# Splitting a stream of expert weight loads between two issuing engines: odd units from ScalarE, even units from SyncE

## The chip, the cores and the metric

The kernel runs on one core of one Trainium2 chip. The metric is the device time of one execution in microseconds (us), lower is better. The profiled execution is a separate one, recorded by the hardware profiler; its trace holds every instruction of the five engines and every packet that the core's 16 DMA engines moved.

## What is computed

One encoder layer over 528 tokens (16 meta tokens and 512 of the input) of width 1024: a retention branch and a long-convolution branch are mixed and added to the tokens, and then a mixture of 16 experts with expert choice follows. Each expert takes the 66 tokens for which its router weight is highest. The part that matters here is the experts:

```
xe  = xn[idx]                                        # 16 experts x 66 tokens x 1024
hid = silu(xe @ w_gate[e]) * (xe @ w_up[e])           # 66 x 2048
ye  = (hid @ w_down[e]) * gate[e]                     # 66 x 1024
out = out.at[idx].add(ye)
```

Everything is float32. The three weight matrices of an expert have 2M elements each, so 24 MiB per expert and 384 MiB in all have to come from HBM, once.

## The kernel before

The first half of the kernel (to about 950 us of the profiled execution) is the two branches and the router. The second half is the experts, and the change is there alone.

**Units.** The weights of the experts are cut into units of 2 MiB. An expert has four units of gate weights, four of up weights and four of down weights. A gate or up unit gives each of the 128 partitions two neighbouring rows of 2048 floats, which lie together in HBM (16 KB); a down unit gives each partition four rows of 1024 floats that lie apart (4 KB each). Unit and expert are named (e, c) in the code, with `MOE_CH` = 12 units to a pass: c = 0 to 3 are the gate units of expert e, c = 4 to 7 its up units, and c = 8 to 11 the down units of expert e - 1, since the down product of an expert runs one pass late. The eight gate and up units of expert 0 come before pass 1 (`high_first`, `low_first`), and the four down units of expert 15 behind pass 15, as (E, 0) to (E, 3) with E = 16.

**Slots and casts.** Units land in a ring of `SLOTS` = 6 float32 buffers `slot`, unit (e, c) in slot (c + 2) % 6. Each unit is then split into two float16 parts: ScalarE (ACT) casts it to the high part `wh` (`high`, L640 to L644), VectorE (DVE) forms the low part `wl` from the float32 unit and `wh` (`low`, L982 to L986), and TensorE (PE) multiplies with both. `wh` and `wl` have `RING` = 4 buffers each. The cast of a unit waits for its landing and for PE to be done with the unit four before it. A slot is free when `low` has been through it, which the semaphore `w_lo` counts.

**Who issues the loads.** All unit loads are issued by SyncE (SP) on its hardware DMA queue (q1 in the profile), in the order of the units:

```
def load(e, c, src, rows):
    sp.wait_ge(S["w_lo"], e * MOE_CH + c - SLOTS - 3)
    sp.dma_start(slot_dst(c + 2, rows), src).then_inc(slot_in[(c + 2) % SLOTS], 16)
```

The wait says that `low` has finished the unit six before this one, whose slot the load overwrites. SP does nothing else in this stage.

**What else is in a pass of ACT and DVE.** ACT's program is in order: twelve casts, and between them `silu` (three activations on PSUM, ahead of the cast of c = 7), `ye_out` and `hidt_high` (behind the cast of c = 3), and `evac_x` (behind the cast of c = 11). DVE runs twelve `low`, with `hidt_low` behind c = 3, and `gated` and `split_x` behind c = 11. GpSimd (POOL) issues one gather (`xg`) and one scatter with accumulation (`h_rows`) for each expert on a queue of its own (q0). ACT's own hardware DMA queue (q10) carries five small loads at the start of the kernel and nothing later.

Of the kernel before, what the change touches and what calls it, by code (L numbers as in the profile page):

```python
# [15 lines left out]
E, FF = 16, 2048  # L16
# [54 lines left out]
MOE_CH = 12  # L71
RING = 4
SLOTS = 6
# [106 lines left out]
def build(nc, A, out, xn2_rows, h_rows):  # L180
    ctx = ExitStack()
    with ctx:
# [12 lines left out]
        S = {n: ctx.enter_context(nc.semaphore("s_" + n)) for n in SEMS}  # L195
        raw_in = [ctx.enter_context(nc.semaphore(f"s_raw_in{i}")) for i in range(3)]
        slot_in = [ctx.enter_context(nc.semaphore(f"s_slot_in{i}")) for i in range(SLOTS)]
# [100 lines left out]
        def gate_src(e, q):  # L298
            return w_gate[e].rearrange("(p k) n -> p k n", k=KD)[:, 2 * q:2 * q + 2, :]

        def up_src(e, q):
            return w_up[e].rearrange("(p k) n -> p k n", k=KD)[:, 2 * q:2 * q + 2, :]

        def down_src(e, q):
            return w_down[e].rearrange("(t p) n -> p t n", p=128)[:, 4 * q:4 * q + 4, :]

        def slot_dst(n, rows):
            return slot[n % SLOTS][:, :].rearrange("p (k n) -> p k n", k=rows)
# [4 lines left out]
        def bank_of(b, base=0):  # L313
            return ps_all[:, base + 512 * b:base + 512 * b + TIL * CAP] if b < 2 else ps_all[:, base + 1024:base + 1024 + 4 * CAP]

        def span_of(t, b):
            return t[:, TIL * CAP * b:min(TIL * CAP * (b + 1), 16 * CAP)]
# [3 lines left out]
        @block.sync  # L321
        def _(sp):

            sp.dma_start(htok[0:NMETA, 0, :], A["meta_tokens"]).then_inc(S["h_tok"], 16)
            sp.dma_start(htok[:, 1:NT, :], A["x"][0].rearrange("(k p) d -> p k d", p=128)).then_inc(S["h_tok"], 16)

            def load_chunk(n):
                if n >= 3:
                    sp.wait_ge(S["raw_lo"], n - 2)
                name, c0 = CHUNKS[n]  # L330
                sp.dma_start(raw[n % 3][:, :, :], w[name][:, :, c0:c0 + CW]).then_inc(raw_in[n % 3], 16)

            def load_first(c):
                src = gate_src(0, c) if c < 4 else up_src(0, c - 4)
                sp.dma_start(slot_dst(c, 2), src).then_inc(slot_in[c % SLOTS], 16)

            for n in range(NCH):
                load_chunk(n)
                if n == 1:
                    sp.dma_start(w4[:, :], A["hy_filt_w4"][0]).then_inc(S["filt_params"], 16)  # L340
                    sp.dma_start(win[:, :, :], A["c_win"][:, :, 0, :]).then_inc(S["win"], 16)
                    sp.dma_start(dft_f[:, :, :, :], A["c_dft_f"]).then_inc(S["dft_fwd"], 16)
                    sp.dma_start(dft_i[:, :, :, :], A["c_dft_i"]).then_inc(S["dft_inv"], 16)
                if n == 7:
                    sp.wait_ge(S["tile_done"], AT[("Y", 0, 3)] + 1)
                    sp.dma_start(win[:, :, :], A["c_win"][:, :, 1, :]).then_inc(S["win"], 16)
                if n == 12:
                    sp.wait_ge(S["tile_done"], AT[("Z", 1, NT - 1)] + 1)
                    sp.dma_start(cosT[:, :], A["c_cos"]).then_inc(S["tables"], 16)
                    sp.dma_start(sinT[:, :], A["c_sin"]).then_inc(S["tables"], 16)  # L350
                    sp.dma_start(utab[:, :], A["c_u"]).then_inc(S["tables"], 16)
                if n >= C_A + 1 and n < C_A + 5:
                    if n == C_A + 1:
                        sp.wait_ge(S["yain_split"], KD)
                    load_first(n - C_A - 1)
                if n == C_B + 2:
                    sp.wait_ge(S["tile_done"], AT[("YA", KD - 1)] + 1)
                    sp.dma_start(h[0:NMETA, 0, :], A["meta_tokens"]).then_inc(S["h_again"], 16)
                    sp.dma_start(h[:, 1:NT, :], A["x"][0].rearrange("(k p) d -> p k d", p=128)).then_inc(S["h_again"], 16)
            sp.wait_ge(S["tile_done"], AT[("YB", KD - 1)] + 1)  # L360
            sp.dma_start(g2b[:, :], A["norm2_g"][0].partition_broadcast(128)).then_inc(S["g2_row"], 16)
            sp.wait_ge(S["tile_done"], AT[("WO", 3, NT - 1)] + 1)
            load_first(4)
            load_first(5)
            for c in (6, 7):
                sp.wait_ge(S["w_lo"], c - SLOTS + 1)
                load_first(c)
            sp.wait_ge(S["rows_landed"], 32)
            sp.dma_start(gfb[:, :], A["final_norm_g"].partition_broadcast(128)).then_inc(S["gf_row"], 16)

            def load(e, c, src, rows):
                sp.wait_ge(S["w_lo"], e * MOE_CH + c - SLOTS - 3)
                sp.dma_start(slot_dst(c + 2, rows), src).then_inc(slot_in[(c + 2) % SLOTS], 16)

            with sp.Fori(1, E) as e:
                for q in range(4):
                    load(e, q, gate_src(e, q), 2)
                for q in range(4):
                    load(e, 4 + q, up_src(e, q), 2)
                for q in range(4):  # L380
                    load(e, 8 + q, down_src(e - 1, q), 4)
            for q in range(4):
                load(E, q, down_src(E - 1, q), 4)
            sp.wait_ge(S["rows_landed"], 32 + 16 * E)
            for k in range(1, NT):
                sp.dma_start(hfin[:, k - 1, :], h_rows[TS[k][0]:TS[k][0] + 128, :]).then_inc(h_back[k - 1], 16)
            for k in range(1, NT):
                sp.wait_ge(S["fin_ready"], k)
                sp.dma_start(out[0, 128 * (k - 1):128 * k, :], hfin[:, k - 1, :]).then_inc(S["out_stored"], 16)
            sp.wait_ge(S["out_stored"], 16 * (NT - 1))  # L390
# [72 lines left out]
        def _(act):  # L463
# [162 lines left out]
            def evac_x(e):  # L626

                act.wait_ge(S["xe_done"], e + 1)
                for b in range(2):
                    src = ps_all[:, 1536 + 512 * b:1536 + 512 * b + 4 * CAP].rearrange("p (k c) -> p k c", k=4)  # L630
                    nc.scalar.activation(xcur[:, 4 * b:4 * b + 4, 0, :], src, ACT.Copy).then_inc(S["xcur_hi"], 1)

            def high_first(c):

                act.wait_ge(slot_in[c % SLOTS], 16 * (c // SLOTS + 1))
                if c >= RING:
                    act.wait_ge(S["chunk_used"], c - RING + 1)
                nc.scalar.activation(wh[c % RING][:, :], slot[c % SLOTS][:, :], ACT.Copy, scale=W_S).then_inc(S["w_hi"], 1)  # L638

            def high(e, c):  # L640

                act.wait_ge(slot_in[(c + 2) % SLOTS], e * 32 + 16 * ((c + 2) // SLOTS))
                act.wait_ge(S["chunk_used"], e * MOE_CH + c - RING - 3)
                nc.scalar.activation(wh[c % RING][:, :], slot[(c + 2) % SLOTS][:, :], ACT.Copy, scale=W_S).then_inc(S["w_hi"], 1)  # L644

            def silu(done):

                act.wait_ge(S["chunk_used"], done)
                for b in range(BANKS):
                    nc.scalar.activation(span_of(sg, b), bank_of(b), ACT.Silu, scale=1.0 / W_S).then_inc(S["psum_free"], 1)  # L650
# [5 lines left out]
            def ye_out(e, done, at):  # L656
                act.wait_ge(S["chunk_used"], done)
                act.wait_ge(S["rows_landed"], e * 16 + 32)
                nc.scalar.activation(ye[:, :], ps_all[0:CAP, at:at + 1024], ACT.Copy, scale=gate[:, bass.ds(e, 1)]).then_inc(S["ye_ready"], 1)  # L659
# [6 lines left out]
            for c in range(2, 8):  # L666
                if c == 7:
                    silu(4)
                high_first(c)
            evac_x(1)  # L670

            def moe(e, second, last):

                for c in range(MOE_CH):
                    if c == 7:
                        silu(e * MOE_CH)
                    high(e, c)
                    if c == 3:
                        if not second:
                            ye_out(e - 2, e * MOE_CH - 4, 3072)  # L680
                        hidt_high(e - 1, hidt)
                if not last:
                    evac_x(e + 1)
# [4 lines left out]
            moe(E - 1, False, True)  # L688
            hidt_high(E - 1, hidt_end)
            for c in range(4):  # L690
                high(E, c)
                if c == 3:
                    ye_out(E - 2, E * MOE_CH - 4, 3072)
# [721 lines left out]
```

## Time and profile before

| | before |
|---|---|
| median of 3 runs | 1984.39 us (1984.2 to 1988.61) |
| profiled execution, its own time | 1983.55 us |
| span of the profiled execution | 1981.7 us |
| mean granted TensorE clock | 0.924 of full speed |
| busy share of the span: PE, DVE, ACT, POOL | 82%, 63%, 50%, 13% |
| queue q1 (SP), all loads of the kernel | 467.94 MB |
| expert stage, in the span | about 953 to 1960 us |

Busy shares are averages over both halves. In the expert stage alone DVE and ACT are much busier than the table says, and so are the DMA engines. The span runs from the first instruction to the last one; the profiled execution's own time is 1.85 us more than its span. "DMA share" of a stretch is the mean busy share of the 16 DMA engines, and it can read a little over 1 since packets overlap at their ends.

### The profile page before, as it was taken

The page shows a single profiled execution, that of the slowest core. Times are in us where ns is not written, and L with a number is a line of the kernel's source. Part 1 is how long each engine was busy: PE and PEld are TensorE (multiplying, and loading weights), DVE is VectorE, ACT ScalarE, POOL GpSimd, SP SyncE. Part 2 cuts the span into 40 slices and gives each one's busy share as a digit, 9 for nine tenths or more (in the row PEclk, how much of TensorE's full clock was granted, in tenths as well). Part 3 has the DMA queues.
Part 4 walks back from the last instruction along what each step waited for, and adds up shares of the span by engine and source line. Part 5 has one row for each costly group of instructions (what it writes and reads, how often), then busy time and mean ns, then how long its engine had stood idle before and what let it go on. Part 6 is the DMA issues. An engine that isn't in the chain of part 4 may idle for free.

```text
span 1981.7 us, 43798 instructions
## 1 busy us (share of the span) xinstructions
PE 1625.5 (82%) x19979; PEld 1225.1 (62%) x19979; DVE 1255.5 (63%) x733; ACT 1000.6 (50%) x622; POOL 263.9 (13%) x137
## 2 busy tenths in 40 slices
PE   4898999898999999984568787778876787777974
PEld 3553773487868888873566565655565565654652
DVE  4423343247235233334699888989889988899884
ACT  4231133132213222222487777777677777777763
POOL 0405041403000000000007301101011000101000
PEclk9799999899999999995789899989899999899987
DMA  9000210112200725122799999999999999999993
GB/s 324 22 22 0 77 58 0 64 44 85 86 0 22 291 94 170 54 79 94 311 361 408 402 410 406 408 412 412 402 403 415 409 409 404 404 416 408 422 406 122
DMA packets 107994, 482.43 MB, mean 243 GB/s; under 512 B 5867, under 2 KB 51243, under 8 KB 91212
## 3 DMA queue, kind: packets, MB, share of 16 engines
q1 hardware_dynamic: 102656, 467.94, 60.0%
q0 software_dynamic: 4704, 12.98, 2.4%
q8 instruction: 66, 1.08, 0.2%
q10 hardware_dynamic: 556, 0.32, 0.1%
q14 instruction: 12, 0.10, 0.0%
HBM read 470.48 MB, written 10.75 MB: 243 GB/s over the span
## 4 chain that ended last, share of the span: by engine, by line
PE 37%; DMA 32%; DVE 14%; ACT 9%; issue 6%; POOL 2%; SPq 0%; ACTq 0%; DVEq 0%; POOLq 0%
PE ps_all L1047 23%; DMA slot<-in_w_exp_gate 15%; DMA slot<-in_w_exp_down 15%; DVE wl L985 8%; ACT wh L644 6%; PE ps_all L1070 5%; PE ps_all L1128 4%; DVE tmp L826 1%; PE ps_all L1114 1%; POOL qk L427 1%; PE ps_all L1232 1%; ACT wh L638 1%; POOL tmp L419 1%; POOL psp L424 1%; DMA xg<-xn_rows,tok 1%
## 5 line engine op out<-in xcount | busy, mean ns | idle before, releaser
L985 DVE SCALAR_TENSOR_TENSOR wl<-slot,wh 128x4096 f16<-128x4096 f32 x184 | 809.2, 4422 | 98.9 <-ACT wh L644 98.6
L644 ACT ACTIVATE wh<-slot 128x4096 f16<-128x4096 f32 x184 | 664.3, 3616 | 223.4 <-DMA slot<-in_w_exp_down 104.1
L1269 PE MATMUL ps_all<-xcur,wl 128*128 128x66 f16 x4096 | 421.7, 198 | 183.7 <-ACT sg L650 103.5
L1269 PEld LDWEIGHTS ps_all<-xcur,wl 128*128 128x128 f16 x4096 | 397.5, 102 | 200.1 <-ACT sg L650 105.1
L1270 PE MATMUL ps_all<-xcur,wh 128*128 128x66 f16 x4096 | 421.4, 199 | 6.5 <-issue 6.5
L1271 PE MATMUL ps_all<-xcur,wh 128*128 128x66 f16 x4096 | 420.7, 200 | 6.5 <-issue 6.5
L1270 PEld LDWEIGHTS ps_all<-xcur,wh 128*128 128x128 f16 x4096 | 397.5, 100 | 6.8 <-issue 6.5
L1271 PEld LDWEIGHTS ps_all<-xcur,wh 128*128 128x128 f16 x4096 | 397.6, 101 | 3.1 <-issue 3.1
L1047 PE MATMUL ps_all<-xnt,wsp 128*128 128x272 f16 (+1 forms) x2688 | 309.8, 278 | 7.0 <-DVE rot L860 5.2
L1047 PEld LDWEIGHTS ps_all<-xnt,wsp 128*128 128x128 f16 x2688 | 264.9, 99 | 52.4 <-issue 8.4
L1283 PE MATMUL ps_all<-wh,hidt 128*66 128x512 f16 x480 | 182.6, 380 | 23.7 <-DVE wl L985 23.4
L719 DVE SCALAR_TENSOR_TENSOR wsp<-raw,wsp 128x2048 f16<-128x2048 f32 x44 | 100.8, 2291 | 136.7 <-ACT wsp L477 136.5
L1285 PE MATMUL ps_all<-wh,hidt 128*66 128x512 f16 x480 | 182.6, 380 | 0.0
L1284 PE MATMUL ps_all<-wl,hidt 128*66 128x512 f16 x480 | 182.4, 380 | 0.0
L447 POOL DMA_INDIRECT h_rows<-ye,tok x16 | 97.9, 6117 | 527.4 <-ACT ye L659 527.4
L477 ACT ACTIVATE wsp<-raw 128x2048 f16<-128x2048 f32 x44 | 83.5, 1901 | 78.7 <-PE ps_all L1047 38.0
L1283 PEld LDWEIGHTS ps_all<-wh,hidt 128*66 128x66 f16 x480 | 53.2, 111 | 80.6 <-issue 35.6
L440 POOL DMA_INDIRECT xg<-xn_rows,tok x16 | 36.7, 2296 | 410.7 <-PE ps_all L1252 360.5
L1285 PEld LDWEIGHTS ps_all<-wh,hidt 128*66 128x66 f16 x480 | 53.4, 111 | 50.8 <-issue 0.7
L1284 PEld LDWEIGHTS ps_all<-wl,hidt 128*66 128x66 f16 x480 | 53.4, 111 | 45.9 <-issue 0.7
L1047 PE MATMUL ps_all<-dft_i,psp 128*128 128x272 f16 (+1 forms) x480 | 65.8, 303 | 11.4 <-POOL psp L424 11.4
L1128 PE MATMUL ps_all<-zt_t,dft_f 128*128 128x512 f16 (+3 forms) x300 | 70.6, 386 | 3.5 <-DVE zt_t L815 3.5
(189 smaller groups left out, 1603.3 us busy)
## 6 DMA issues: line engine op xcount, KB each, us to landing
slot<-in_w_exp_gate SPq DMA_DIRECT2D x64, 2048.0 KB, 23.7
slot<-in_w_exp_up SPq DMA_DIRECT2D x64, 2048.0 KB, 21.4
slot<-in_w_exp_down SPq DMA_DIRECT2D x64, 2048.0 KB, 22.6
raw<-in_w_in SPq DMA_DIRECT2D x32, 1024.0 KB, 5.9
raw<-in_w_ret_out SPq DMA_DIRECT2D x4, 1024.0 KB, 13.1
raw<-in_w_hy_out SPq DMA_DIRECT2D x4, 1024.0 KB, 7.7
raw<-in_w_o SPq DMA_DIRECT2D x4, 1024.0 KB, 5.3
dft_f<-in_c_dft_f SPq DMA_DIRECT2D x1, 2640.0 KB, 18.3
```

The lines of the kernel that those rows point to most:

```text
L644: nc.scalar.activation(wh[c % RING][:, :], slot[(c + 2) % SLOTS][:, :], ACT.Copy, scale=W_S).then_inc(S["w_hi"], 1)
L719: nc.vector.scalar_tensor_tensor(wsp[n % 3][:, 1, :, :], raw[n % 3][:, :, :], W_S, wsp[n % 3][:, 0, :, :], ALU.mult, ALU.subtract).then_in ...
L985: nc.vector.scalar_tensor_tensor(wl[c % RING][:, :], slot[(c + 2) % SLOTS][:, :], W_S, wh[c % RING][:, :], ALU.mult, ALU.subtract).then_in ...
L1047: last = nc.tensor.matmul(pair(n, c, c + b - a, p), l, r[:, a:b], start=i == 0, stop=i == len(terms) - 1)
L1070: last = nc.tensor.matmul(pair(n, 0, CW, p), l, r, start=i == 0, stop=i == 3 * KD - 1)
L1128: last = nc.tensor.matmul(pair(n, 512 * a, 512 * a + 512, fp), l, r, start=i == 0, stop=i == 3 * NT - 1)
L1269: nc.tensor.matmul(dst, lo, xcur[:, k, 0, :], start=k == 0 and t % TIL == 0, stop=False, skip_group_check=True)
L1270: nc.tensor.matmul(dst, hi, xcur[:, k, 0, :], start=False, stop=False, skip_group_check=True)
L1271: last = nc.tensor.matmul(dst, hi, xcur[:, k, 1, :], start=False, stop=k == KD - 1, skip_group_check=True)
L1283: nc.tensor.matmul(dst, l[0], wh[i][:, f:f + 512], start=t == 0, stop=False)
L1284: nc.tensor.matmul(dst, l[0], wl[i][:, f:f + 512], start=False, stop=False)
L1285: last = nc.tensor.matmul(dst, l[1], wh[i][:, f:f + 512], start=False, stop=t == 15)
```

## The change

SP issues the loads of even c only. The loads of odd c are issued by ACT, on ACT's own hardware queue, from the middle of its program: ahead of the cast of an odd unit c it issues the load of unit c + 2; ahead of the cast of c = 11 it issues (e + 1, 1), or (E, 1) in the last pass. (1, 1) is issued ahead of the last cast of expert 0's units, behind a `silu`, and (E, 3) ahead of the cast of (E, 1). The slots, the semaphores, the counts waited for, the sources and the sizes are the same as before. DVE's, PE's and POOL's programs are the same.

```diff
             with sp.Fori(1, E) as e:
-                for q in range(4):
+                for q in (0, 2):
                     load(e, q, gate_src(e, q), 2)
-                for q in range(4):
+                for q in (0, 2):
                     load(e, 4 + q, up_src(e, q), 2)
-                for q in range(4):
+                for q in (0, 2):
                     load(e, 8 + q, down_src(e - 1, q), 4)
-            for q in range(4):
+            for q in (0, 2):
                 load(E, q, down_src(E - 1, q), 4)
...
+            def load_odd(e, c):
+                act.wait_ge(S["w_lo"], e * MOE_CH + c - SLOTS - 3)
+                if c < 4:
+                    src, rows = gate_src(e, c), 2
+                elif c < 8:
+                    src, rows = up_src(e, c - 4), 2
+                else:
+                    src, rows = down_src(e - 1, c - 8), 4
+                act.dma_start(slot_dst(c + 2, rows), src).then_inc(slot_in[(c + 2) % SLOTS], 16)
+
+            def load_end(q):
+                act.wait_ge(S["w_lo"], E * MOE_CH + q - SLOTS - 3)
+                act.dma_start(slot_dst(q + 2, 4), down_src(E - 1, q)).then_inc(slot_in[(q + 2) % SLOTS], 16)
...
             for c in range(2, 8):
                 if c == 7:
                     silu(4)
+                    load_odd(1, 1)
                 high_first(c)
...
                 for c in range(MOE_CH):
                     if c == 7:
                         silu(e * MOE_CH)
+                    if c % 2 and c < MOE_CH - 2:
+                        load_odd(e, c + 2)
+                    elif c % 2 and not last:
+                        load_odd(e + 1, 1)
+                    elif c % 2:
+                        load_end(1)
                     high(e, c)
...
             for c in range(4):
+                if c == 1:
+                    load_end(3)
                 high(E, c)
```

## Rows read from the trace of the kernel before

**Rows 1.** Busy time by stretch: us, then each engine's, granted clock, DMA share, GB/s.

```profile
995.00:1004.00 9.00, 2.06 (x38) 2.07 (x39) 6.73 (x2) 9.00 (x3) 0.00 (x0) 0.57 0.47 154
1004.00:1075.00 71.00, 60.97 (x1218) 50.02 (x1216) 71.00 (x23) 60.02 (x25) 25.15 (x2) 0.93 1.00 407
1075.00:1930.00 855.00, 663.52 (x11822) 508.69 (x11819) 759.34 (x246) 633.89 (x258) 99.14 (x26) 0.93 1.01 409
```

**Rows 2.** The chain that ended last, 1075 to 1930 us, by line.

```profile
by line: DMA slot<-in_w_exp_gate 35.8%; DMA slot<-in_w_exp_down 34.6%; DVE wl L985 15.9%; ACT wh L644 11.4%; issue 2.2%; SPq L373 0.2%; DVE hid L993 0.2%; DVE hidt L997 0.1%; ACTq L643 0.1%; ACT hidt_end L654 0.0%
```

**Rows 3.** Costliest groups: busy us, mean ns | idle before, releaser; the cast.

```profile
L644 ACT ACTIVATE wh<-slot 128x4096 f16<-128x4096 f32 x184 | 664.3, 3616 | 223.4 <-DMA slot<-in_w_exp_down 104.1
```

**Rows 4.** ACT in order of time, part of one pass: start, us, instruction, idle before.

```profile
1405.07 3.62 ACT L644 ACTIVATE wh<-slot 128x4096 f16<-128x4096 f32 x1 [1.50 <-DMA slot<-in_w_exp_down]
1410.18 3.62 ACT L644 ACTIVATE wh<-slot 128x4096 f16<-128x4096 f32 x1 [1.49 <-DMA slot<-in_w_exp_down]
1417.76 3.62 ACT L644 ACTIVATE wh<-slot 128x4096 f16<-128x4096 f32 x1 [3.96 <-DMA slot<-in_w_exp_down]
1421.29 0.66 ACT L631 ACTIVATE xcur<-ps_all 128x264 f16<-128x264 f32 x2
1422.82 3.62 ACT L644 ACTIVATE wh<-slot 128x4096 f16<-128x4096 f32 x1 [0.88 <-DMA slot<-in_w_exp_gate]
1427.72 3.62 ACT L644 ACTIVATE wh<-slot 128x4096 f16<-128x4096 f32 x1 [1.28 <-DMA slot<-in_w_exp_gate]
...
1455.71 1.15 ACT L650 ACTIVATE sg<-ps_all 128x396 f32<-128x396 f32 x3
```

**Rows 5.** DVE in order of time: four `low` in a row, and what follows c = 11.

```profile
1015.79 17.43 DVE L985 SCALAR_TENSOR_TENSOR wl<-slot,wh 128x4096 f16<-128x4096 f32 x4
...
1425.75 1.38 DVE L993 SCALAR_TENSOR_TENSOR hid<-ps_all,sg 128x396 f32<-128x396 f32 x3
1427.05 0.76 DVE L974 TENSOR_TENSOR xcur<-ps_all,xcur 128x264 f16<-128x264 f32 x2
```

**Rows 6.** All instructions on `slot`: one load issue (ns), and issue to landing.

```profile
L373 SPq DMA_DIRECT2D slot<-in_w_exp_gate x60: 332/340/4277, 963.3 to 1854.6; - x60
...
DMA to landing us min/median/max: 7.3/22.6/25.6
```

**Rows 7.** DMA packets in 1424 to 1427 us (gate, up), and 1395 to 1400 us (down).

```profile
DMA packets 91, 1.31 MB, mean 437 GB/s; under 512 B 11, under 2 KB 11, under 8 KB 11
...
DMA packets 522, 2.07 MB, mean 415 GB/s; under 512 B 16, under 2 KB 16, under 8 KB 522
```

**Rows 8.** DMA queues in 6.0 to 6.5 us: packets, MB, share of 16 engines.

```profile
q1 hardware_dynamic: 42, 0.17, 88.0%
q10 hardware_dynamic: 36, 0.02, 12.2%
```

**Rows 9.** DMA queues in 1387 to 1390 us.

```profile
DMA packets 130, 1.16 MB, mean 386 GB/s; under 512 B 30, under 2 KB 30, under 8 KB 69
...
q1 hardware_dynamic: 64, 1.00, 78.9%
q0 software_dynamic: 66, 0.16, 27.1%
```

**Rows 10.** ACT in order of time, start of the expert stage.

```profile
973.82 3.63 ACT L638 ACTIVATE wh<-slot 128x4096 f16<-128x4096 f32 x1
...
993.62 14.13 ACT L644 ACTIVATE wh<-slot 128x4096 f16<-128x4096 f32 x4
...
1027.63 14.14 ACT L644 ACTIVATE wh<-slot 128x4096 f16<-128x4096 f32 x4 [0.60 <-PE ps_all L1271]
```

**Rows 11.** ACT, casts of c = 11 in the last two passes.

```profile
1856.57 3.62 ACT L644 ACTIVATE wh<-slot 128x4096 f16<-128x4096 f32 x1 [1.49 <-DMA slot<-in_w_exp_down]
...
1917.35 3.62 ACT L644 ACTIVATE wh<-slot 128x4096 f16<-128x4096 f32 x1 [1.47 <-DMA slot<-in_w_exp_down]
```

## The prediction

> **What bounds the kernel now.** I read the busy time by stretch first. From 1075 to 1930 us the 16 DMA engines are full (share 1.01, 409 GB/s), while the busiest compute engine, DVE, works 759 of 855 us [rows 1]. The chain that ended last agrees: 70% of that stretch is landing of weights, and 27% the low and high split in between [rows 2]. The groups show the cast waiting 223 us, most of it for landings [rows 3]. ACT in order of time shows how tight it is: down units are cast 5.11 us apart, gate units 4.90 us apart, each cast 3.6 us, and the wait of 1.3 to 1.5 us before each is for the landing [rows 4]. So in this stage time is packets divided by what the DMA engines carry, and a change of issuers can do two things: change that rate, or leave the engines without work. Before 1075 us the engines have one gap, 995 to 1004 us (share 0.47) [rows 1], and casts wait for PE.
>
> **What is removed.** SP loses half its issues, 0.34 us each, before a landing that comes 22.6 us later (median) [rows 6]. Nobody waits for SP, since this lead hides it: 0 us. The few of its issues that take up to 4.3 us [rows 6] are hidden by the same lead, and become fewer or not, at 0.
>
> **What is added to ACT.** 92 issues (7 or 8 units in 15 passes, and the end). I price one like SP's, 0.34 us [rows 6]: 31 us of ACT time. Lower bound 0 for each; upper bound 0.5 us, if waits and setup are counted. While ACT waits 1.3 to 1.5 us before most casts [rows 4] this is hidden. It counts only where casts run back to back (below). The `w_lo` wait is no new one: the cast behind it needs PE to be done with the same unit.
>
> **What moves: when odd units are issued.** SP issues a unit when `low` is done with the unit six before. ACT issues it ahead of the cast of the unit two before. With units 5.1 us apart the lead shrinks from 22.6 us to two units and what the cast waits, 10 to 12 us. A load alone takes 7.3 us from issue to landing [rows 6], of which 4.9 us are its packets [rows 4], so 2.4 us are start and finish. Two loads that share the engines fairly need about 9.8 + 2.4 = 12.2 us. This is just enough or 1 us too late, as long as sharing is fair in bytes.
>
> **Is it fair?** A gate or up unit is moved in packets of 16 KB (1.31 MB in 80 large packets), a down unit in packets of 4 KB (2.07 MB in some 506) [rows 7]. By unit time that is 4.90/8 = 0.61 us for a 16 KB packet on one of 16 engines, and 5.11/32 = 0.16 us for a 4 KB one. Where SP's and ACT's queues were both full, at 6.0 to 6.5 us, 42 packets of 4 KB of q1 went beside 36 of 0.5 KB of q10 [rows 8]: one for one, whatever their size. POOL's scatter beside gate units shows the same kind of turn: its 36 or so 4 KB packets beside 61 of 16 KB [rows 9], where turns by bytes would let four pass for each. So I take turns by packet. A down unit that competes with gate units then gets 0.16/(0.16 + 0.61) = 21% of the engines' time. That happens once a pass: c = 11, the last down unit, sits on ACT's queue, while SP's queue behind c = 10 holds gate units c = 0, 2, 4 of the next expert.
>
> The Trainium skill (DMA: Bandwidth & Descriptors, "Issuing engines are not separate DMA queues") says that DMAs issued by several engines run on the same 16 DMA engines and interleave, and that this saves only the sequencer's issue time. By this alone the sum would be 0 and the time 1984; the row on packets of unequal size makes it 98 us.
>
> **The loop that results, for one pass**, from the start of cast 11 (t = 0), which waits for its landing. Casts back to back take 3.53 us (14.13/4) [rows 10].
> (a) Casts 11, 0, 1, 2, `evac_x` 0.66 [rows 4] and one issue: load 5 is issued at 14.12 + 0.66 + 0.34 = 15.1.
> (b) It shares with load 6, which SP issues when `low` of c = 0 is done: 3.53 + 4.36 + 1.38 + 0.76 + 4.36 = 14.4 [rows 5]. Both are 16 KB, so 12.2 us: cast 5 at 27.3.
> (c) Casts 5 to 8, `silu` 1.15 [rows 4] and an issue or two: load 11 is issued at 27.3 + 14.1 + 1.15 + 0.5 = 43.0.
> (d) Ahead of it on ACT's ring is c = 9 and beside it c = 10, both down. From 27.3 on the engines move 7, 8, 9 and 10, 4.90 + 3 x 5.11 = 20.2 us, and some POOL packets (1 us, my estimate from the landing gap of 7.6 instead of 5.1 us at 1417.76 [rows 4], half of which I leave to other moments): done at 48.5, 5.5 us behind 11's issue. Then c = 11 meets three gate units: while these take 3 x 4.90 = 14.7 us of engine time, 11 gets 14.7 x 0.16/0.61 = 3.9 of its 5.11 us, then the last 1.2 alone: 19.8. With 0.8 us to finish it lands at 43.0 + 5.5 + 19.8 + 0.8 = 69.1.
> A check from the other side: at t = 0 all three even slots are landed and not yet cast. Only load 1 is queued, then 3 (issued at 8.1 by ACT) and 6 (14.4). 6 lands at 14.4 + 7.3 = 21.7, where three units back to back would take 14.7: 7 us of empty DMA engines in a pass, against the 6.1 that 69.1 gives. I take 69.1, between 67.5 and 70.
>
> **The sum.** Cast 11 of pass 1 is now the fourth of four from 1027.63, at 1038.2 [rows 10]; that of pass 14 is at 1856.57 [rows 11]: 13 passes in 818.4, 62.95 each. After: 13 x 69.1 = 898.3, so +79.9 (59 to 92). Start: in pass 1 load 11 goes out ahead of cast 9, at 1031.3, and takes the same 5.5 + 19.8 + 0.8 less about 1 (little is queued), 25 us: 1056.3 instead of 1038.2, +18 (12 to 20). The later issue of (1, 1), (1, 3) and (1, 5) lies inside this, since casts there wait for PE. End: pass 15 is 60.8 now [rows 11]; there 11 meets down units on the other queue and is not starved, and (E, 3), issued late, is cast last anyway: +1 (0 to 4). What follows the last `low` is unchanged: 0. Together 79.9 + 18 + 1 = +98.9, against the profiled execution's own 1983.55, which is 0.8 below the median of the runs: 2082. The likeliest case's own range is 2055 to 2100.
>
> **Rivals.**
> *Fair sharing* (15%): the engines share by bytes, or 16 KB packets are cut up before the turn is taken. Then no pass is longer; 12.2 us of landing fits the lead within 1 us. Left are the start, where (1, 3) is issued only at 997.2, ahead of the second of four casts [rows 10], so that the gap of [rows 1] starts some 6 us earlier, and the end, where (E, 0) goes ahead of (15, 11), up to 5.1 us: 1984 + 6 + 5 = 1995. Against it is [rows 8].
> *Turns by group* (12%): turns are one for one over longer groups than a packet. A gate unit has only 8 packets on an engine, 4.9 us, a down unit 32; if a turn is up to 16 packets, c = 11 gets 2.6/(2.6 + 4.9) = 34%, (d) is 5 us shorter, a pass 64: 13 x 1.1 + 13 + 1 = 28, 2012. The half microsecond of [rows 8] can't tell this from single packets. In the Trainium skill the same page's "Queues, rings and completion order" has an engine drain a packet of about 9 to 17 descriptors from one ring before it switches.
> *Faster* (5%): two rings fill each other's gaps, so that down units move at the 4.90 us of gate units, 0.21 x 4 = 0.8 us a pass or 13 us in all, less 6 at the start: 1977. It decides only if sharing is fair too, and from 0.4 us a pass on. Against it: share 1.01 and packets end to end already.
> *No change* (3%): the issue time alone matters, and the two ends cancel: 1984.
> *Worse* (3%): ACT's issues take up to 4.3 us, as a few of SP's do [rows 6], 4 us or more in a pass: above 2130. But SP has four units outstanding (22.6 us of 5.1 each), ACT two at most.
> The rest, 62%, is my forecast. The range 1994 to 2100 takes in the first two rivals. 0.3% (6 us) is what measurement can tell: faster 5%, same 4%, slower 91%.
>
> **What would show each step.** In the profile after: casts of c = 11 some 69 us apart; down loads from ACT landing 24 to 26 us after issue at the longest, gate loads from SP in 12 to 20; before cast 11 ACT idle some 13 us for a landing, and little idle elsewhere but before cast 5 and cast 9; two dips of DMA share just behind cast 11; about 375 GB/s over the stage instead of 409; q10 with some 190 MB. I am wrong if odd down loads land in 12 us, for then sharing is fair, or if the share stays at 1.0 all through a pass.

## The result and the profile after

The changed kernel takes 1998.51 us (median of 5 runs, 1991.39 to 2002.52) against 1984.39 us (5 runs, 1983.16 to 1988.61). The ratio is 1.0062, with a 95% interval of 1.0038 to 1.0086: slower, by 14 us in the medians. The forecast was 2082 us, 98 us slower. The sign was right; the size was seven times too large. The time lies in the stated range of 1994 to 2100 us, near its lower end, but outside the 2055 to 2100 us that the forecast gave its likeliest case. The profiled execution after took 1991.39 us by its own time, 7.8 us more than the one before, and was the fastest of the five, so its trace holds a little over half of the loss.

Busy time by stretch, after, the columns as in [rows 1]:

```profile
995.00:1004.00 9.00, 4.33 (x95) 4.34 (x96) 9.00 (x3) 9.00 (x3) 0.00 (x0) 0.56 1.03 376
1004.00:1075.00 71.00, 55.17 (x1039) 42.20 (x1035) 62.72 (x20) 54.52 (x23) 5.76 (x2) 0.95 1.01 409
1075.00:1930.00 855.00, 670.09 (x11890) 506.44 (x11891) 751.54 (x243) 624.25 (x257) 121.75 (x25) 0.94 1.01 406
```

The DMA engines are as full from 1075 to 1930 us as before (share 1.01), and move 406 GB/s instead of 409. The forecast had them empty for 6 us of every pass. That is the first thing to see: the big term of the sum is not there. The gap that the kernel before had at 995 to 1004 us is not there either; there the engines are full (share 1.03), since the shortage came earlier, from 953 to 995 us (298 GB/s instead of 353).

The group of the cast, and issue to landing of all unit loads:

```profile
L644 ACT ACTIVATE wh<-slot 128x4096 f16<-128x4096 f32 x184 | 657.7, 3612 | 245.2 <-DMA slot<-in_w_exp_down 183.5
```

```profile
DMA to landing us min/median/max: 7.3/14.5/24.4
```

The cast's waits for down units rose from 104 to 184 us [rows 3], while its idle time as a whole rose by 22 us only. So one kind of unit comes late and the others come early. ACT in order of time shows which (ACTq rows are load issues):

```profile
1403.26 3.62 ACT L644 ACTIVATE wh<-slot 128x4096 f16<-128x4096 f32 x1 [0.56 <-PE ps_all L1296]
1403.47 0.39 ACTq L655 DMA_DIRECT2D slot<-in_w_exp_down  x1
1409.44 7.12 ACT L644 ACTIVATE wh<-slot 128x4096 f16<-128x4096 f32 x2 [2.57 <-DMA slot<-in_w_exp_down]
1413.09 0.35 ACTq L655 DMA_DIRECT2D slot<-in_w_exp_gate  x1
1426.22 3.62 ACT L644 ACTIVATE wh<-slot 128x4096 f16<-128x4096 f32 x1 [9.65 <-PE ps_all L1310]
1426.98 0.35 ACTq L655 DMA_DIRECT2D slot<-in_w_exp_gate  x1
1429.75 0.65 ACT L631 ACTIVATE xcur<-ps_all 128x264 f16<-128x264 f32 x2
1430.29 3.62 ACT L644 ACTIVATE wh<-slot 128x4096 f16<-128x4096 f32 x1
1435.91 3.62 ACT L644 ACTIVATE wh<-slot 128x4096 f16<-128x4096 f32 x1 [2.01 <-DMA slot<-in_w_exp_gate]
1436.22 0.34 ACTq L655 DMA_DIRECT2D slot<-in_w_exp_up  x1
```

The cast at 1426.22 is that of c = 11, the last down unit. Its load was issued at 1403.47 and took 22.8 us; ACT stood still for 9.65 us before it. (The wait is put down to PE here, as in two other passes; in the rest of passes 3 to 14, where it is 7.6 to 13.8 us, it is put down to the down unit's landing, and the next experiments show that it is the landing.) The DMA queues in 1414 to 1416 us, while c = 11 on ACT's queue meets gate units on SP's:

```profile
q1 hardware_dynamic: 36, 0.59, 69.6%
q10 hardware_dynamic: 41, 0.17, 20.6%
```

41 packets of 4 KB against 36 of 16 KB, and 20.6% of the engines' time: this is the forecast's one for one and its 21%. Over the longer stretch from 1412 to 1418 us it is nearly the same (13 of q1's packets are tiny ones):

```profile
q1 hardware_dynamic: 136, 2.02, 79.4%
q10 hardware_dynamic: 143, 0.59, 24.0%
```

Counts alone don't show the order of turns. The packet records have no engine number, but a packet that follows another on its engine can be told by its start, 3 or 4 ns before the other's end. In the 124 stretches of 1 us between 1075 and 1930 us in which SP's 16 KB packets meet ACT's 4 KB packets, the one found behind a 16 KB packet of SP is a 4 KB packet of ACT in 854 cases and another of SP's in 20, no more than chance hits would give. So one packet ends the turn.

Now look at when the loads go out. The load issued at 1426.98 is c = 3. In ACT's program it stands behind the cast of c = 11, behind `evac_x` and behind the cast of c = 0, which ends at 1433.9. It was issued 0.76 us after the cast of c = 11 began. The next one, c = 5, went out 0.3 us after the cast of c = 1 began, ahead of the end of that cast and of the whole cast of c = 2. I had both behind the last finished cast: at 8.1 and 15.1 us from the start of cast 11, instead of 0.8 and 10.0.

The account of this one trace, by casts of c = 11:

```profile
1048.66 3.62 ACT L644 ACTIVATE wh<-slot 128x4096 f16<-128x4096 f32 x1 [6.09 <-DMA slot<-in_w_exp_down]
...
1870.63 3.62 ACT L644 ACTIVATE wh<-slot 128x4096 f16<-128x4096 f32 x1 [8.10 <-DMA slot<-in_w_exp_down]
...
1926.37 3.62 ACT L644 ACTIVATE wh<-slot 128x4096 f16<-128x4096 f32 x1 [3.11 <-PE ps_all L1310]
```

Pass 1: 1048.66 against 1038.17, +10.5. Passes 2 to 14: 822.0/13 = 63.23 us each against 62.95 [rows 10, 11], +3.6 in all. Pass 15: 55.7 against 60.8, -5.0. Together the last cast of c = 11 is 9.0 us later, and the span 7.9 us longer. These steps mix lost time with changed order: c = 11 is cast late from pass 1 to pass 14 because other units go ahead of it, and in pass 15, where it meets down units only, 5.0 us come back. What was really lost, and when, is read from the bytes moved, in the section on the prediction.

### The profile page after: what moved, and what is told of

The parts are those of the page before. It is cut to its first block, busy times and chain, and to the rows that moved or that the text cites. A ratio compares the mean times of both kernels' runs of the same rounds, so it can differ in the third digit from the quotient of the medians.

```text
span 1989.6 us, 43783 instructions
## 1 busy us (share of the span) xinstructions
PE 1636.4 (82%) x19979; PEld 1220.9 (61%) x19979; DVE 1248.6 (63%) x733; ACT 990.9 (50%) x622; POOL 267.0 (13%) x137
## 4 chain that ended last, share of the span: by engine, by line
PE 39%; DMA 24%; DVE 17%; issue 10%; ACT 7%; POOL 2%; ACTq 0%; DVEq 0%; SPq 0%; POOLq 0%
PE ps_all L1072 23%; DMA slot<-in_w_exp_down 18%; DVE wl L1010 9%; PE ps_all L1095 5%; DMA slot<-in_w_exp_gate 5%; PE ps_all L1153 4%; ACT wh L644 4%; DVE tmp L851 1%; PE ps_all L1294 1%; PE ps_all L1296 1%; PE ps_all L1139 1%; PE ps_all L1295 1%; POOL qk L427 1%; PE ps_all L1257 1%; ACT wh L638 1%
## 5 line engine op out<-in xcount | busy, mean ns | idle before, releaser
L644 ACT ACTIVATE wh<-slot 128x4096 f16<-128x4096 f32 x184 | 657.7, 3612 | 245.2 <-DMA slot<-in_w_exp_down 183.5
L1294 PE MATMUL ps_all<-xcur,wl 128*128 128x66 f16 x4096 | 411.7, 196 | 131.2 <-DVE wl L1010 80.7
L1294 PEld LDWEIGHTS ps_all<-xcur,wl 128*128 128x128 f16 x4096 | 390.4, 101 | 145.4 <-issue 86.4
L1295 PE MATMUL ps_all<-xcur,wh 128*128 128x66 f16 x4096 | 411.6, 196 | 7.2 <-issue 7.2
L1296 PE MATMUL ps_all<-xcur,wh 128*128 128x66 f16 x4096 | 411.3, 198 | 4.7 <-issue 4.7
L1295 PEld LDWEIGHTS ps_all<-xcur,wh 128*128 128x128 f16 x4096 | 390.6, 99 | 8.2 <-issue 7.3
L1296 PEld LDWEIGHTS ps_all<-xcur,wh 128*128 128x128 f16 x4096 | 390.6, 99 | 4.2 <-issue 4.2
L1308 PE MATMUL ps_all<-wh,hidt 128*66 128x512 f16 x480 | 191.2, 398 | 75.6 <-DVE wl L1010 75.6
L1309 PE MATMUL ps_all<-wl,hidt 128*66 128x512 f16 x480 | 190.8, 398 | 0.0
L1310 PE MATMUL ps_all<-wh,hidt 128*66 128x512 f16 x480 | 190.3, 396 | 0.0
L440 POOL DMA_INDIRECT xg<-xn_rows,tok x16 | 94.4, 5897 | 450.7 <-PE ps_all L1277 400.8
L447 POOL DMA_INDIRECT h_rows<-ye,tok x16 | 43.5, 2717 | 492.3 <-ACT ye L675 492.3
L1310 PEld LDWEIGHTS ps_all<-wh,hidt 128*66 128x66 f16 x480 | 55.7, 116 | 55.7 <-issue 9.3
## 6 DMA issues: line engine op xcount, KB each, us to landing
slot<-in_w_exp_gate SPq DMA_DIRECT2D x34, 2048.0 KB, 13.8
```

The source lines that it names most:

```text
L1294: nc.tensor.matmul(dst, lo, xcur[:, k, 0, :], start=k == 0 and t % TIL == 0, stop=False, skip_group_check=True)
L1295: nc.tensor.matmul(dst, hi, xcur[:, k, 0, :], start=False, stop=False, skip_group_check=True)
L1296: last = nc.tensor.matmul(dst, hi, xcur[:, k, 1, :], start=False, stop=k == KD - 1, skip_group_check=True)
L1308: nc.tensor.matmul(dst, l[0], wh[i][:, f:f + 512], start=t == 0, stop=False)
L1309: nc.tensor.matmul(dst, l[0], wl[i][:, f:f + 512], start=False, stop=False)
L1310: last = nc.tensor.matmul(dst, l[1], wh[i][:, f:f + 512], start=False, stop=t == 15)
```

## The experiments

The ratio of each is to the kernel before, on the same chip. "Theory" and "rival" are as stated ahead of each run. The edits are cuts of the whole ones.

**Take ACT's lead away.** One more wait puts each load really behind the casts ahead of it:

```diff
+                    if c % 2:
+                        act.wait_ge(S["w_hi"], e * MOE_CH + c - 4)
                     if c % 2 and c < MOE_CH - 2:
                         load_odd(e, c + 2)
```

(and the same before `load_odd(1, 1)` and `load_end(3)`).

> The changed kernel, but ACT issues each odd load only when the casts ahead of it in its program are finished (one more wait on ACT's count of finished casts). Theory A (the loads went out 4 to 7 us earlier than forecast, because ACT's sequencer passes the wait and the DMA issue while the casts ahead still run, and this lead kept the DMA engines full): with the lead taken away the forecast loop appears, passes of 66 to 69 us, 2030 to 2085 us, and DMA gaps behind the cast of c = 11. Theory B (the lead never mattered, since the rings share fairly or hold enough anyway): within 6 us of the changed kernel's 1998.

Measured: 2039.81 us, ratio 1.0270 (1.0255 to 1.0285), +54 us. One pass of it, from one cast of c = 11 to the next:

```profile
1520.33 3.62 ACT L644 ACTIVATE wh<-slot 128x4096 f16<-128x4096 f32 x1 [7.97 <-DMA slot<-in_w_exp_down]
...
1528.26 0.35 ACTq L655 DMA_DIRECT2D slot<-in_w_exp_gate  x1
...
1536.17 0.34 ACTq L655 DMA_DIRECT2D slot<-in_w_exp_up  x1
...
1546.91 7.12 ACT L644 ACTIVATE wh<-slot 128x4096 f16<-128x4096 f32 x2 [1.20 <-DMA slot<-in_w_exp_up]
...
1565.43 0.39 ACTq L655 DMA_DIRECT2D slot<-in_w_exp_down  x1
1570.69 7.12 ACT L644 ACTIVATE wh<-slot 128x4096 f16<-128x4096 f32 x2 [5.50 <-DMA slot<-in_w_exp_down]
...
1586.45 3.62 ACT L644 ACTIVATE wh<-slot 128x4096 f16<-128x4096 f32 x1 [8.64 <-DMA slot<-in_w_exp_down]
```

The loads of c = 3 and c = 5 now go out 7.9 and 15.8 us after cast 11 (forecast 8.1 and 15.1), cast 5 starts at 26.6 (27.3), load 11 is issued at 45.1 (43.0), and the pass is 66.1 us (69.1). Busy time by stretch shows the DMA gap just behind cast 11, which the changed kernel doesn't have:

```profile
1525.00:1530.00 5.00, 1.98 (x10) 0.85 (x9) 5.00 (x6) 4.20 (x2) 0.00 (x0) 1.00 0.82 305
1530.00:1535.00 5.00, 3.89 (x19) 1.78 (x16) 5.00 (x4) 5.00 (x2) 0.00 (x0) 1.00 0.87 370
1535.00:1540.00 5.00, 4.01 (x123) 3.89 (x124) 5.00 (x2) 4.32 (x2) 0.00 (x0) 1.00 0.88 321
```

So the forecast's loop is real and its steps hold, once ACT issues as I had assumed. Theory A stands, B falls. Of the 98 us forecast, 44 don't come even so, some 39 of them from the loop (13 passes of 66.1 instead of 69.1 us): step (d), from the issue of 11 to its landing, takes 21.0 us instead of 26.1, while the steps ahead of it take 2.1 us more than forecast. SP's issues say why (d) is short:

```profile
1562.06 9.03 SPq L373 DMA_DIRECT2D slot<-in_w_exp_gate  x2
1583.13 0.33 SPq L373 DMA_DIRECT2D slot<-in_w_exp_up  x1
```

Only two gate units are issued beside c = 11; SP's next one goes out at 1583.13, 3.3 us before cast 11, right behind `low` of c = 10, which ends at 1583.1. I had let it meet three.

**The same late issue, on one ring.** Here ACT issues all units, even and odd, two ahead, each behind finished casts; SP issues none of passes 1 to 15:

```diff
+                    act.wait_ge(S["w_hi"], e * MOE_CH + c - 4)
+                    if c < MOE_CH - 2:
+                        load_odd(e, c + 2)
+                    elif not last:
+                        load_odd(e + 1, c - MOE_CH + 2)
```

> All loads of passes 1 to 15 and the end by ACT, each only when the casts ahead of it are finished: the late issue of run e1, but one ring in the order of the units. If the 55 us of e1 need both (a down unit starved on one ring while late issue leaves nothing on the other), the passes are back at 63 us here: some 10 us of late start more than with all loads on ACT, 1993 to 2005 us. If late issue alone makes them, 2030 us or more, passes of 65 to 66.

Measured: 1991.02 us, ratio 1.0036 (1.0025 to 1.0048). A little under the 1993 to 2005 us of the first theory, and far from the 2030 us of the other. Its stretch and its landings:

```profile
1075.00:1930.00 855.00, 660.67 (x11862) 511.00 (x11859) 758.61 (x243) 635.97 (x257) 84.02 (x26) 0.93 1.01 408
```

```profile
DMA to landing us min/median/max: 10.8/12.2/13.7
```

12 us from issue to landing are enough, and no unit takes more than 13.7. The late issue alone costs the steady passes nothing (62.9 us each); the 54 us need both, the late issue and the second ring. That it is the starving of c = 11 that matters in the second ring is argued: late issue on two rings with packets of one size was not tried.

**All loads from ACT, without the wait.** The kernel above without its `w_hi` waits.

> All unit loads of passes 1 to 15 and of the end, even and odd, are issued by ACT two units ahead, SP issues none of them: one ring again, in the order of the units, with ACT's short lead. Theory A, part two (the 14 us come from having two rings: down units pushed behind gate units, order turned round at the end, 16 KB packets slowed): gone here, 1984 to 1990 us, ratio 1.000 to 1.003, and no wait of 10 us before the cast of c = 11. Rival (the 14 us come from the shorter lead): 1998 us or more, since now all units have it.

Measured: 1993.04 us, ratio 1.0039 (1.0026 to 1.0053). Between the two expectations. The steady passes are the old ones, but the start is not:

```profile
953.00:1004.00 51.00, 35.93 (x890) 35.14 (x889) 43.53 (x17) 35.78 (x18) 1.90 (x2) 0.77 0.64 241
1075.00:1930.00 855.00, 655.64 (x11883) 505.64 (x11879) 757.80 (x243) 636.99 (x258) 77.65 (x26) 0.93 1.01 409
```

From 953 to 1004 us the kernel before moves 318 GB/s, this one 241: 51 x 77/409 = 9.6 us of DMA work left for later. ACT stands before the gather of expert 1 until about 990 us, and what it would issue waits with it.

**The end in order.** In pass 15 and behind it SP issues all units but (15, 1), ACT none.

> The changed kernel up to pass 14; in pass 15 and at the end all loads but that of (15, 1) are issued by SP in the order of the units, as before. If the units that overtake (15, 11) cost the end 5 to 7 us: 1990 to 1993 us, ratio 1.003. If the loss is spread evenly over the passes (slower packets): 1997, ratio 1.006.

Measured: 1999.02 us, ratio 1.0061 (1.0039 to 1.0083). The end is not where the loss is. Cast 11 of pass 15 does come sooner behind that of pass 14 (50.8 us instead of 55.7), but the last four casts then start 14.7 us behind it instead of 10.4.

**The start in order.** Two kernels in which SP issues all of pass 1; from (2, 1) on the odd units come from ACT (first), or from (2, 0) on all units (second):

```diff
-            with sp.Fori(1, E) as e:
+            for q in range(4):
+                load(1, q, gate_src(1, q), 2)
...
+            with sp.Fori(2, E) as e:
```

(this is of the first; in the second the whole `Fori` goes.)

> The changed kernel, but all loads of pass 1 come from SP in the order of the units, as before; ACT issues odd units from (2, 1) on. If the loss is mostly the start (ACT stands before the gather of expert 1 and can't issue (1, 3) and (1, 5), so that the DMA engines run empty sooner): 1986 to 1991 us, ratio 1.001 to 1.003. If the loss comes from two rings in the steady passes: 1996 us, ratio 1.005 or more.

> All loads of pass 1 come from SP, all later ones, even and odd, from ACT two units ahead: one ring at a time, no late loads at the start. If the loss of the run with all loads on ACT (ratio 1.0039) is the start alone: 1984 us, ratio 1.000 within 0.001. If the shorter lead costs something in each pass: ratio 1.003 again.

Measured: 1995.18 us, ratio 1.0044 (1.0027 to 1.0061), and 1989.92 us, ratio 1.0022 (1.0012 to 1.0031). Both gain some 3.5 us on their kernels with the late start, and neither reaches what the theory of the start alone gave. In the second, the one place where two rings meet shows the whole effect once more, at the handover in pass 1 (ACT in order of time, then busy time by stretch):

```profile
1034.57 0.33 ACTq L652 DMA_DIRECT2D slot<-in_w_exp_gate  x1
1048.26 3.62 ACT L641 ACTIVATE wh<-slot 128x4096 f16<-128x4096 f32 x1 [10.21 <-DMA slot<-in_w_exp_down]
1048.57 1.11 ACTq L652 DMA_DIRECT2D slot<-in_w_exp_gate  x2
```

```profile
1044.00:1048.00 4.00, 4.00 (x20) 2.10 (x19) 3.55 (x1) 0.00 (x0) 4.00 (x1) 1.00 0.43 181
```

ACT's gate units overtake SP's (1, 11), ACT waits 10.21 us for that down unit, and since it is ACT that would issue the next loads, the engines run dry: 4 x 0.57 = 2.3 us. They are short of work until about 1060 us. The stretch around it, this kernel first and the kernel before second:

```profile
1040.00:1075.00 35.00, 28.42 (x349) 17.97 (x346) 30.64 (x12) 26.39 (x11) 13.30 (x2) 1.00 0.91 373
1040.00:1075.00 35.00, 31.74 (x467) 22.50 (x465) 35.00 (x14) 27.61 (x12) 22.82 (x2) 0.95 1.01 412
```

35 x 39/409 = 3.3 us of DMA work is lost at the handover, most of the 4 us that this kernel is slower.

**Packets of one size.** The changed kernel and the kernel before, both with gate and up units taken in four pieces of 4 KB a partition. The weights are permuted by this, so the experts' products are other numbers; the work is the same.

```diff
-            return w_gate[e].rearrange("(p k) n -> p k n", k=KD)[:, 2 * q:2 * q + 2, :]
+            return w_gate[e].rearrange("k (h n) -> (k h) n", h=2).rearrange("(t p) n -> p t n", p=128)[:, 4 * q:4 * q + 4, :]
```

> The changed kernel with gate and up units fetched in pieces of 4 KB instead of 16 KB (other rows of the weights in each partition, so the experts' products are of permuted weights; the work of each engine is the same). All packets are then of one size. If turns go by packet, the last down unit is no longer starved: wait before the cast of c = 11 below 5 us instead of 10 to 13, longest landing about 16 us instead of 24. If turns don't go by packet, that wait stays. Time: units move at 5.1 us each, so some 8 x 0.2 x 15 = 25 us more than the changed kernel, 2010 to 2030; compared with the one-ring kernel of the same packets it should be 0 to 8 us slower.

> The kernel before with gate and up units in pieces of 4 KB (permuted weights, as in the run beside it): the base for that run. 1984 + 8 x 0.21 x 15 = 2009 us.

Measured: 2010.19 us, ratio 1.0131 (1.0113 to 1.0150), and 2003.28 us, ratio 1.0106 (1.0090 to 1.0122). The first expectation is met but for two figures (longest landing 22.7 us, not 16; longest wait before c = 11 5.4 us, not below 5). The second expected 2009 us and is 6 us too high: smaller packets cost 19 us, not 25. The waits of the two-ring kernel, 1075 to 1930 us (total, times, longest):

```profile
ACT wh L644 <- DMA slot<-in_w_exp_down: 102.0, 26, 5.4
ACT wh L644 <- DMA slot<-in_w_exp_gate: 74.9, 26, 4.2
```

```profile
ACT wh L644 <- DMA slot<-in_w_exp_down: 170.6, 38, 13.8
```

The second fence is the same view of the changed kernel. With equal packets the longest wait falls from 13.8 to 5.4 us and gate units wait like down units, as turns by packet would have it. Two rings still cost 7 us against one ring, with nobody starved. The profiles put it at the start: from 953 to 1004 us 284 against 321 GB/s, 4.7 us of DMA work, and from 1075 to 1930 us 400 GB/s in both. Pass 1's cast of c = 11 is at 1048.4 against 1036.9 us, and the 14 passes behind it take 64.1 against 64.3 us each.

**Larger packets for down units.** Four kernels take down units in 16 KB pieces, which needs the hidden features in another order. In two of them PE reads the gate and up weights with a stride of 16, in two ACT and DVE put them in order (strided read in the cast and in `low`).

```diff
-            return w_down[e].rearrange("(t p) n -> p t n", p=128)[:, 4 * q:4 * q + 4, :]
+            return w_down[e].rearrange("(p t) n -> p t n", t=16)[:, 4 * q:4 * q + 4, :]
...
-                        hi, lo = wh[i][:, f:f + 128], wl[i][:, f:f + 128]
+                        hi, lo = wh[i][:, f:f + 2033:16], wl[i][:, f:f + 2033:16]
```

> The kernel before with down units fetched in pieces of 16 KB (four neighbouring rows of a partition), and the columns of gate and up weights taken by PE with a stride of 16 so that the result is the reference's. All packets are 16 KB: down units should come 4.90 us apart instead of 5.11, 4 x 0.21 x 15 = 13 us less: 1972 us, if strided weight loads do not slow PE (its 82% leaves room) and the stage stays bound by packets. If PE loads strided weights slower, no gain or a loss, with casts waiting for PE.

> The changed kernel with down units in 16 KB pieces, as in the run beside it: all packets of one size on two rings. No starved unit: wait before the cast of c = 11 below 5 us. If a starved unit is what costs the change its 14 us, within 4 us of the one-ring kernel of the same packets; if two rings cost by themselves (slower packets), 6 us or more above it.

> The kernel before with down units in 16 KB pieces; the columns of gate and up weights are put in the order that this needs by the split itself (ACT and DVE read the float32 unit with a stride of 16 and write in order), so that PE reads its weights without a stride. Same result as the reference. If ACT and DVE keep their 3.62 and 4.42 us with a strided read: down units 4.90 us apart instead of 5.11, 1972 us, ratio 0.994. If the strided read slows DVE by more than 0.5 us a unit: slower than 1984 us.

> The changed kernel with down units in 16 KB pieces by the same means. All packets are of one size, so the last down unit is not starved: wait before the cast of c = 11 below 5 us. Time: that of the one-ring kernel beside it plus the start's loss, 5 to 10 us; if DVE is slowed by the strided read, both are bound by DVE and equal.

Measured: 2110.33 us (1.0645) on one ring and 2114.52 (1.0652) on two with PE's stride; 2253.41 (1.1358) and 2255.97 (1.1355) with the strided split. Each pair is equal within its intervals, so they say nothing of rings: another engine has become the bound. With PE's stride PE is busy for 848 of the 855 us, with the strided split DVE for 845. The groups of the one-ring kernels show what grew:

```profile
L1271 PEld LDWEIGHTS ps_all<-xcur,wh 128*128 128x128 f16 x4096 | 697.4, 170 | 0.0
```

```profile
L993 DVE SCALAR_TENSOR_TENSOR wl<-slot,wh 128x4096 f16<-128x4096 f32 x184 | 1136.2, 6245 | 22.2 <-ACT wh L651 22.2
L651 ACT ACTIVATE wh<-slot 128x4096 f16<-128x4096 f32 x184 | 1089.5, 6034 | 51.1 <-PE ps_all L1293 26.8 <-PE ps_all L1279 24.3
```

No version beat the kernel before.

## Why the prediction was wrong, step by step

**What bounds the kernel: right.** The stage follows the DMA engines in both kernels (share 1.01).

**Turns by packet: right.** 41 packets beside 36, 20.6% of the engines' time where 21% was forecast (24.0% over 6 us), and the wait cut to 5.4 us when packets are equal. The rival of turns by group expected 34%. The Trainium skill (DMA: Bandwidth & Descriptors, "Queues, rings and completion order") lets a ring drain some 9 to 17 descriptors before the turn passes; if a record of the trace is a descriptor, the order of the records, where the turn passes behind a single 16 KB packet in 854 of 874 cases, doesn't agree with that for these two rings. The rival of fair sharing came closest in time (1995 us) with a mechanism that the trace refutes: c = 11 is starved in passes 3 to 14 and waits 7.6 to 13.8 us. The time was near for another reason, and that the stated range holds the result is luck: its lower end was there for that rival alone.

**When odd units are issued: wrong, and this is the step that failed.** I wrote that the lead shrinks to two units less the cast, and in steps (a) and (c) let each load wait for the end of the cast ahead. ACT's sequencer does the semaphore wait and the DMA issue while casts that it has handed over are still running, up to two casts and an `evac_x` ahead. What holds it, as far as these runs show, is only the waits ahead of it in the program. At cast 11 those were all met, so load 3 left at 0.8 us instead of 8.1 (0.4 to 0.8 us in every pass), and the 7 us of empty engines in a pass, 80 of the 98 us, never came. The prediction named its own sign for this: it is wrong if the share stays at 1.0 all through a pass. Putting the loads behind finished casts brought 54 us; taking the second ring away as well took them back. The loop was mis-sized besides: 66.1 us where the forecast had 69.1, from (d), 5.1 us too long, with two gate units to meet and not three.

With the engines never empty, a late c = 11 costs nothing by itself: the gate units that overtook it are there when it comes, and ACT casts them back to back.

**The start: +18 forecast.** The cast of c = 11 in pass 1 is 10.5 us late, but most of this is order and not loss. The bytes moved from 953 to 1004 us, in the kernel before, in the changed one, and in the run with the end in order, whose loads are those of the changed kernel up to here:

```profile
953.00:1004.00 51.00, 31.56 (x816) 30.46 (x815) 40.00 (x16) 35.10 (x17) 1.90 (x2) 0.83 0.80 318
953.00:1004.00 51.00, 32.17 (x872) 31.15 (x872) 42.27 (x17) 37.36 (x18) 1.90 (x2) 0.85 0.81 312
953.00:1004.00 51.00, 31.67 (x784) 30.71 (x784) 36.48 (x15) 31.63 (x16) 1.90 (x2) 0.80 0.71 269
```

That is 0.7 us of DMA work behind in the one execution and 51 x 49/409 = 6.1 us in the other. So the start costs anything from 0.7 to 6 us in these two, and the changed kernel's profiled execution, the fastest of its five, hardly paid it. Moving the start back to SP gained 0.18% on two rings (1.0062 to 1.0044) and 0.17% on one (1.0039 to 1.0022); each step is about as large as its intervals, but both agree: 3 to 4 us.

**The rest: a term put at nothing.** The sum let the engines move as many bytes a microsecond as before. From 1075 to 1930 us the changed kernel moves 406 GB/s at the same share of 1.01, and the kernel with two rings from pass 2 moves 404; the kernels with one ring move 408 and 409. The stretch with 404:

```profile
1075.00:1930.00 855.00, 666.31 (x11829) 503.94 (x11826) 743.47 (x241) 621.92 (x256) 117.85 (x25) 0.93 1.01 404
```

3/409 of 855 us is 6 us, most of the 7.9 us that the trace after is longer. The packet records show where: the 16 KB packets on SP's queue take 645 ns on average in both kernels with two rings, against 630 before, and 6656 x 15 ns/16 engines is again 6 us; the 4 KB packets take what they took (163 and 165 ns). What makes them longer was not tried. Two rings against one, both with the start in order, is 1.0044 to 1.0022, some 4 us with intervals that overlap a little, which agrees. The 4 us by which even the kernel with one ring from pass 2 is slower than the one before are, to within 1 us, the 3.3 us of its handover.

**The issues themselves:** 0.34 to 0.39 us each, near the 0.34 priced, and hidden, since ACT still idles 245 us before its casts. They are six in each of 15 passes and two at the end; the total of 92 was right, "7 or 8" a pass was not.

## What to carry to other kernels

A DMA issue in ACT's program did not wait for the operations ahead of it to finish, only for the semaphore waits ahead of it: place it by the waits, not by the work. Two queues with packets of different size give the smaller packets the smaller share, packet for packet, so a stream that must arrive in order should stay on one queue. Packets of one size on both queues end the starving, but here they still cost 7 us against one queue. And before a stall is priced, ask whether the shared engine is ever empty: where it isn't, a unit that comes late only changes places with one that comes early.

## What the runs showed of the hardware

- ACT's queue issued a load 0.76 us after a cast began, with two evacuations and a cast between them in the program: the sequencer ran at least four instructions ahead. It did so in every pass, 0.4 to 0.8 us after that cast began.
- Where 16 KB packets of one ring met 4 KB packets of another, the turn passed behind a single 16 KB packet in 854 of 874 cases found.
- Weight loads of 128 x 128 float16 with a stride of 16 elements took 170 ns instead of 100, and the matmuls behind them 229 instead of 199.
- A strided float32 read (stride 16) in two units of three raised the mean of `low` from 4.42 to 6.25 us and of the cast from 3.62 to 6.03: about 7.2 us for a strided unit on either engine, (3 x 6.25 - 4.42)/2 and (3 x 6.03 - 3.62)/2.
- On two rings with 4 KB and 16 KB packets the engines moved 0.7 to 1.2% less at the same busy share (406 and 404 GB/s against 409), and the 16 KB packets on SP's queue took 645 ns on average instead of 630; with 4 KB packets alone one and two rings both moved 400 GB/s.
